# A hybrid layer on one core: linear attention placed between the last six in-projection slots, sliding attention within the first eight, gate sums ahead of them

## The chip, the core and the metric

The kernel runs on one core of a Trainium2 chip. Its engines run side by side, each through its own program in order, and meet in semaphores: TensorE multiplies matrices (its weight loads are a row of their own, PEld, in the profile), VectorE (DVE) and ScalarE (ACT) work elementwise, GpSimd (POOL) does a little elementwise work and issues transfers, SyncE (SP) issues transfers. The metric is the device time of one execution in microseconds (us), the median of the runs shown.

## What is computed

A block of two models. The first is one layer on 512 tokens of width 1024 whose mixer has three parts: sliding-window attention with 8 heads, an RWKV-7 recurrence with 4 heads, and gated linear attention with 4 heads. All three read the same normalised input. The second model, two more layers with full attention and feed-forward parts, is untouched here. Of the first layer's reference, what matters:

```python
h = _rmsnorm(x, g_pre) * (1.0 + scale[:, None]) + shift[:, None]
proj = h @ w_in                                   # 25 groups of 128 columns with the low-rank one
aq, ak, av, ag, rkv, rg, gq, gkk, gv, gg = jnp.split(proj, ...)
attn = _sliding_window_attention(aq, ak, av, sinks) * jax.nn.silu(ag)
rkv = rkv + (_shift(rkv) - rkv) * mu_rkv          # "token mix"
rwkv = _rwkv7_mixer(h, *jnp.split(rkv, 3, axis=-1), ...) * jax.nn.silu(rg)
gla = _gla_mixer(h, gq, gkk, gv, gk1, gk2, gk_b, gla_norm_w) * jax.nn.silu(gg)
y = jnp.concatenate([attn, rwkv, gla], axis=-1) @ w_out
return x + gate[:, None] * _rmsnorm(y, g_post)    # gate = c_act @ ada_w + ada_b, last third

# in _gla_mixer, for chunks of 64 tokens
b = jnp.cumsum(g_c, axis=2)
A = jnp.einsum('bhid,bhjd,bhijd->bhij', q_c, k_c, jnp.exp(diff))   # diff = b_i - b_j, causal
o = A @ v_c + jnp.einsum('bhid,bhdv->bhiv', q_c * jnp.exp(b), S)
```

## The kernel before

The whole program is one function, `build`, with a block of code for each engine. Nothing schedules it: the order on an engine is the order in which its block is written, and every meeting is a semaphore wait written by hand. Weights are full 32-bit numbers; each is split into a rounded high half and the rest (a low half), and each product is made of three matmuls (`three`, L2011 to L2013: high times high, high times low, low times high).

**The in-projection** has 24 slots after the low-rank one, of one weight tile of 128 columns each: `in1(item, g)` for g = 1 to 24. A slot is eight k-steps of three matmuls of 128x512. SyncE loads tiles into a ring (`refill`, L1947). ScalarE makes a tile's high half when the slot two before it is used (`ahead`, `weight_high`, L1203), VectorE then makes its low half (`weight_low`, L1490), and TensorE waits for that (`split_slot`). ScalarE also evacuates each slot's bank (`late` for the last fourteen, L2509); from item 17 on two banks take turns.

**Sliding attention** has 16 units u of a block of 128 queries and a pair of heads; the first four look at 128 keys, the others at 256. TensorE does `s1_step(u)`: transposes of unit u's probabilities (L2139), scores of unit u+1 (L2127), values of unit u-1 (L2153). Between, VectorE does `s1_max` (maximum L2823, then small operations to L2830), ScalarE `s1_exp` (L2559, L2561), VectorE `s1_normalise` (L2837 to L2840). `s1_gate` (L2846) takes the output. A step stands after every seventh k-step of slots 11 to 24. VectorE's loop over u also holds the low halves, the six token mixes (L2792, L2793; u = 2 to 7), the scan of the decay (L2865, u = 3) and the eight gate sums (`gate_sum`, L2801; u = 8 to 15), each over a tile of 512 KB that SyncE loads beside the ring's refills. A low half stands between the normalising of u and the maximum of u+1.

**Linear attention** is made in seven levels and a diagonal, since the decay between two tokens is a product of distances to the edges of blocks of 1, 2, 4, ... 64 tokens. For each level GpSimd computes distances (`g_distance`, L2442, L2443), ScalarE exponentiates them (`g_power`, L2582), VectorE multiplies queries and keys (`g_level`, L2877, L2878), TensorE makes 16 small matmuls of 32 rows, 4 chunks by 4 heads (`g_scores`, L2211; L2213 for the diagonal), and VectorE copies what belongs to the level under a mask (`g_take`, L2891; L2895 for the diagonal). Two sets of four PSUM banks take turns. Besides there are turned values and keys, chunk states (`g_state`), and the outputs in four blocks (`g_outputs`, L2225, L2228), which ScalarE copies (L2631). All of this stands behind the last slot. In its gaps stands **the recurrence's pointwise work** (key norms L2179, exponentials L2618, L2619, L2628, products L2947 to L2957). It ends in `r_inputs` 6, on which the recurrence's products wait (L2273), which VectorE masks in eight banks (`masked`, L2964).

The two lines that set the pace of steps and of late slots before:

```python
                if (at + k) % 7 == 6:                       # TensorE
                    s1_step((at + k) // 7)
            while 8 * split + 7 <= 7 * u + 6 and split < 14:   # VectorE, ahead of s1_max(u + 1)
                weight_low(ve, S_IN1 + 11 + split + SPLIT)
```

## Time and profile before

| | us |
|---|---|
| median of 3 runs | 1761.24 |
| lowest, highest | 1759.0, 1761.84 |
| the profiled execution | 1760.94 |
| its span | 1759.2 |
| its mean granted TensorE clock | 0.982 |

The profile is of one execution. Its times run from the span's start. The stretch that the change touches is from about 50 us (gate sums) and 106.4 us (slot 11) to about 271 us (the recurrence's level chain). "Released by" is inferred from semaphores. A TensorE row's busy time overlaps with its neighbours', so start to start is what a matmul takes in a row of them.

### The profile page before, as it was taken

The numbers are of one execution on the slowest core, as the hardware profiler recorded it, in microseconds if no ns is written. First come the engines' busy times: TensorE is split into PE (matmuls) and PEld (weight loads), VectorE is DVE, ScalarE is ACT, GpSimd is POOL, SyncE is SP. The second block draws the span as 40 slices with busy tenths as digits, with TensorE's granted clock in tenths as the row PEclk, the third lists the DMA queues.
The fourth block names the chain that finished last, engine by engine and source line by source line (L and its number), as shares of the span: only waits on it lengthen the run. The fifth ranks groups of instructions, "written<-read, shape, count | busy, mean of one in ns | idle before, by whom it ended". The sixth has DMA issues, their size and how long they took to land.

```text
span 1759.2 us, 32981 instructions
## 1 busy us (share of the span) xinstructions
PE 1701.1 (97%) x14287; PEld 1535.3 (87%) x14287; DVE 915.6 (52%) x1808; ACT 645.7 (37%) x1098; POOL 354.1 (20%) x466
## 2 busy tenths in 40 slices
PE   7999989989999999999999999999999999999997
PEld 3777779869988789999999998799769999999886
DVE  5347694445355654565652113788782556556002
ACT  3354442243145544222222224322683422222223
POOL 0001102001210012222222222343012222222221
PEclk9999979898999999999999999999999999999999
DMA  8521400126973358988889999699306888888996
GB/s 309 160 73 60 180 2 4 53 55 150 228 170 73 73 119 183 186 182 180 184 181 187 196 201 200 146 208 218 84 2 138 175 188 183 180 186 183 197 205 150
DMA packets 81648, 265.39 MB, mean 151 GB/s; under 512 B 11632, under 2 KB 15472, under 8 KB 81376
## 3 DMA queue, kind: packets, MB, share of 16 engines
q0 software_dynamic: 59040, 214.98, 57.7%
q1 hardware_dynamic: 18448, 42.52, 7.1%
q10 hardware_dynamic: 4016, 5.78, 1.1%
q8 instruction: 113, 1.85, 0.4%
q14 instruction: 31, 0.25, 0.0%
HBM read 251.44 MB, written 2.10 MB: 144 GB/s over the span
## 4 chain that ended last, share of the span: by engine, by line
PE 79%; DVE 3%; DMA 3%; ACT 2%; issue 1%; ACTq 0%; POOL 0%; DVEq 0%
PE banks L661 21%; PE banks L662 20%; PE banks L663 20%; PE banks L2273 3%; DMA w_lo<-in_weights 2%; PE banks L798 1%; DMA w_hi<-in_weights 1%; PE banks L729 1%; PE banks L713 1%; PE banks L2011 1%; PE banks L751 1%; PE banks L836 1%; PE banks L2013 1%; PE banks L2012 1%; PE banks L1072 1%
## 5 line engine op out<-in xcount | busy, mean ns | idle before, releaser
L661 PE MATMUL banks<-hn_hi,w_hi 128*128 128x264 f32 (+2 forms) x2168 | 624.7, 288 | 4.7 <-DMA w_lo<-in_weights 4.0
L662 PE MATMUL banks<-hn_lo,w_hi 128*128 128x264 f32 (+2 forms) x2168 | 617.1, 285 | 0.0
L663 PE MATMUL banks<-hn_hi,w_lo 128*128 128x264 f32 (+2 forms) x2168 | 616.4, 284 | 0.0
L1209 ACT ACTIVATE w_lo<-w_hi 128x1024 fp32r<-128x1024 f32 x202 | 214.1, 1060 | 720.5 <-DMA w_hi<-in_weights 712.5
L661 PEld LDWEIGHTS banks<-hn_hi,w_hi 128*128 128x128 f32 x2168 | 409.3, 189 | 17.0 <-issue 12.2
L662 PEld LDWEIGHTS banks<-hn_lo,w_hi 128*128 128x128 f32 x2168 | 410.4, 189 | 0.6 <-issue 0.2
L663 PEld LDWEIGHTS banks<-hn_hi,w_lo 128*128 128x128 f32 x2168 | 408.2, 188 | 0.3
L1154 POOL DMA_DIRECT2D w_hi<-in_weights x205 | 113.5, 554 | 881.2 <-PE banks L663 794.0
L1161 POOL DMA_DIRECT2D w_lo<-in_weights x205 | 183.2, 896 | 171.4 <-ACT w_lo L1209 122.2
L661 PE MATMUL banks<-a_hi,w_hi 128*128 128x264 f32 (+1 forms) x506 | 160.6, 317 | 1.9 <-DVE u_in L1758 0.8
L662 PE MATMUL banks<-a_lo,w_hi 128*128 128x264 f32 (+1 forms) x506 | 160.7, 318 | 0.0
L663 PE MATMUL banks<-a_hi,w_lo 128*128 128x264 f32 (+1 forms) x506 | 160.6, 317 | 0.0
L661 PEld LDWEIGHTS banks<-a_hi,w_hi 128*128 128x128 f32 x506 | 95.3, 188 | 9.7 <-DVE u_in L1758 1.0
L663 PEld LDWEIGHTS banks<-a_hi,w_lo 128*128 128x128 f32 x506 | 95.2, 188 | 6.7
L662 PEld LDWEIGHTS banks<-a_lo,w_hi 128*128 128x128 f32 x506 | 95.0, 188 | 6.6
L1758 DVE TENSOR_TENSOR u_in<-banks,rs 128x528 f32<-128x528 f32 x44 | 31.2, 708 | 98.3 <-PE banks L663 88.9
L1760 DVE TENSOR_TENSOR u_in<-banks,rs 128x516 f32<-128x516 f32 x44 | 30.6, 696 | 98.1 <-PE banks L663 91.3
L1490 DVE TENSOR_TENSOR ring_r<-ring,ring_r 128x1024 fp32r<-128x1024 f32 x32 | 39.6, 1238 | 76.5 <-ACT ring_r L1203 76.5
L2012 PE MATMUL banks<-h_r,ring_r 128*128 128x512 f32 x192 | 76.0, 396 | 0.0
L661 PE MATMUL banks<-o_hi,w_hi 128*128 128x264 f32 (+1 forms) x256 | 73.3, 286 | 1.3 <-DMA w_lo<-in_weights 0.7
L662 PE MATMUL banks<-o_lo,w_hi 128*128 128x264 f32 (+1 forms) x256 | 72.5, 283 | 0.0
L663 PE MATMUL banks<-o_hi,w_lo 128*128 128x264 f32 (+1 forms) x256 | 72.4, 283 | 0.0
(452 smaller groups left out, 2752.0 us busy)
## 6 DMA issues: line engine op xcount, KB each, us to landing
w_hi<-in_weights POOLq DMA_DIRECT2D x205, 512.0 KB, 5.2
w_lo<-in_weights POOLq DMA_DIRECT2D x205, 512.0 KB, 7.3
ring<-in_weights SPq DMA_DIRECT2D x48, 512.0 KB, 4.7
arena<-arena ACTq DMA_DIRECT2D x64, 66.0 KB, 5.4
arena<-arena SPq DMA_DIRECT2D x64, 66.0 KB, 4.0
arena<-in_gate_w SPq DMA_DIRECT2D x8, 512.0 KB, 3.5
h<-in_xT SPq DMA_DIRECT2D x2, 1024.0 KB, 6.4
arena<-in_alibi SPq DMA_DIRECT2D x1, 1024.0 KB, 6.4
```

The source lines that it names most:

```text
L661: mm(o, w[0][:, j, :], x[0][:, k, lo:hi], start=first, stop=False)
L662: mm(o, w[0][:, j, :], x[1][:, k, lo:hi], start=False, stop=False)
L663: ins_ = mm(o, w[1][:, j, :], x[0][:, k, lo:hi], start=False, stop=last)
L713: last = mm(psum[:, 2 * (v % 2) + c, at], qs[r, p, b * P:(b + 1) * P], kz[r, p, 0:keys(b)], start=True, stop=True)
L1154: g.dma_start(split_at(n)[0], ins["weights"][n]).then_inc(hi_loaded[w_turn(n)[0]], 16)
L1161: g.dma_start(split_at(n)[1], ins["weights"][n], accum_op=ALU.add).then_inc(lo_summed[w_turn(n)[0]], 16)
L1209: nc.scalar.activation(split_at(n)[1], split_at(n)[0].bitcast(F32), ACT.Copy, scale=-1.0).then_inc(S["w_negated"], 1)
L1490: nc.vector.tensor_tensor(ring_lo(n), ring_slot(n), ring_hi(n).bitcast(F32), ALU.subtract).then_inc(S["w_split_d"], 1)
L1758: V.tensor_tensor(halves(u_in[:, g % 4, 2:T2 + 2]), pair(g), rs2, ALU.mult).then_inc(S["u_evac"], 1)
L1760: V.tensor_tensor(halves(u_in[:, g % 4, KEEP + 2:T2 + 2]), kept_pair(g), halves(rs[:, KEEP:T2]), ALU.mult).then_inc(S["u_evac"], 1)
L2012: mm(out, w[0][:, k, :], x_lo, start=False, stop=False)
L2273: last = mm(out(s), lhs[r], rhs[r], start=start, stop=stop)
```

## The change

What it does:

- *TensorE:* an attention step stands after every fourth k-step, so that 16 steps end with slot 18 (`beside(p)`, p counts k-steps from slot 11). Between the k-steps of slots 19 to 24 stand the turned values and keys, the states, the key norms and their spreading, and the scores of each level, in two pieces of two heads each, one k-step apart (`G_SCORES_AT`). All levels use banks 0 to 3: a piece waits until the same heads of the level before are copied.
- *VectorE:* the attention loop keeps the maximum, normalising, gating, four token mixes (u = 3, 5, 7, 9), the scan (u = 4) and eight low halves, of which each stands ahead of every second maximum. Behind it come linear attention and the pointwise work with the six other low halves and two mixes between. `masked(0)` to `masked(3)` stand behind the norm of linear attention, since its output `g_o` now lies where the masked products go.
- *ScalarE:* five `g_power` in the loop (u = 8 to 12), the late slots' high halves and evacuations between the pointwise work, and both SiLU behind the last evacuation and ahead of the output copies.
- *GpSimd:* five distances as soon as the scan is there, instead of three; the zeroing behind the last maximum.
- *Gate sums:* VectorE does them beside the low halves of slots 1 to 10, and SyncE loads their tiles beside the refills there.
- *Layout:* several tiles move; the recurrence's v columns (two slots) are projected after q, k and v of linear attention.

The diff, cut:

```diff
-    ch = Carve(hn_raw, KT * (T2 + 1))
-    g_at = ch.take(4, T1)
-    g_kd = ch.take(T1)
-    g_o = ch.take(2, T1)
+    g_o = arena[:, front:front + 2 * T1].rearrange("p (j t) -> p j t", j=2)
...
+    BESIDE = 64
+    G_SCORES_AT = (67, 73, 78, 83, 88, 93, 98, 103)
...
         for n in range(S_IN1 + 6, S_IN1 + 10):
             refill(n)
+            if n > S_IN1 + 6:
+                gate_tile(n - S_IN1 - 7)
...
-        def g_scores(lv):
+        def g_scores(lv, pair):
...
-            elif lv:
-                pe.wait_ge(S["g_taken"], 2 * (lv - 1))
...
+            else:
+                pe.wait_ge(S["g_taken"], 2 * (lv - 1) + pair + 1)
             for c in range(4):
-                for hd in range(4):
+                for hd in (2 * pair, 2 * pair + 1):
...
+        def beside(p):
+            if p == 0:
+                s1_scores(0)
+            if p < BESIDE and p % 4 == 3:
+                s1_step(p // 4)
+            if p == 66:
+                s1_values(15)
+            if p in (68, 69):
+                g_values_turned(p - 68)
+            if p == 71:
+                g_keys_turned()
+            if p == 75:
+                g_states()
+            if p == 81:
+                key_norms()
+            if p == 92:
+                key_norms_spread()
+            for pair in range(2):
+                if p - pair in G_SCORES_AT:
+                    g_scores(G_SCORES_AT.index(p - pair), pair)
...
-        for lv in range(3):
+        for lv in range(5):
             g_distance(lv)
...
+        for j in range(11, 14):
+            late(j)
+        act.wait_ge(S["in1_evac"], ITEMS)
+        A(rgate, rgate, ACT.Silu)
+        A(ggate, ggate, ACT.Silu)
         for c in range(4):
             act.wait_ge(S["g_ops"], c + 1)
...
         for g in range(1, 7):
             weight_low(ve, S_IN1 + g + SPLIT)
+            if g >= 3:
+                gate_sum(g - 3)
...
-            while 8 * split + 7 <= 7 * u + 6 and split < 14:
+            while 8 * split + 7 <= 4 * u + 3:
                 weight_low(ve, S_IN1 + 11 + split + SPLIT)
...
-            if 2 <= u < 8:
-                token_mix(u - 2)
-            elif u >= 8:
-                gate_sum(u - 8)
+            if u in (3, 5, 7, 9):
+                token_mix((u - 3) // 2)
...
-        masked(0)
-        masked(1)
...
+        for b in range(4):
+            masked(b)
         first_level(0)
...
-        _groups(rkv), _groups(gq), _groups(gk), _groups(gv), _groups(rg), _groups(gg),
+        _groups(rkv[:, :512]), _groups(gq), _groups(gk), _groups(gv), _groups(rkv[:, 512:]), _groups(rg), _groups(gg),
```

TensorE, the scores of linear attention. Before, they stand behind the last slot, with nothing between the levels but their waits:

```order
L2211 MATMUL banks<-arena 128x64 x16
...
L2211 MATMUL banks<-arena 128x64 x16
...
L2211 MATMUL banks<-arena 128x64 x80
L2213 MATMUL banks<-arena 128x128 x16
```

In the changed kernel, a piece of eight stands between k-steps of three (L2024 to L2026 are the three matmuls, L2205 the scores, L2246 the states), here in slot 20:

```order
L2205 MATMUL banks<-arena 128x64 x8
L2024 MATMUL banks<-mix_r,ring_r 128x512
L2025 MATMUL banks<-h_r,ring_r 128x512
L2026 MATMUL banks<-mix_r,ring_r 128x512
L2205 MATMUL banks<-arena 128x64 x8
L2024 MATMUL banks<-mix_r,ring_r 128x512
L2025 MATMUL banks<-h_r,ring_r 128x512
L2026 MATMUL banks<-mix_r,ring_r 128x512
L2246 MATMUL banks<-arena 128x256 x3
```

A level's sixteen matmuls have become two pieces of eight between projection matmuls.

ScalarE, ahead of the output copies of linear attention. Before (L2621 the key factor, L2623 and L2624 the two SiLU, L2626 the square root, L2628 an exponential, L2631 the output copies):

```order
L2621 ACTIVATE arena<-arena,small,cols 128x512 x2
L2623 ACT_TABLE_LOAD
L2623 ACTIVATE arena<-arena 128x1024
L2624 ACTIVATE arena<-arena 128x1024
L2626 ACT_TABLE_LOAD
L2626 ACTIVATE arena<-arena 128x16
L2628 ACT_TABLE_LOAD
L2628 ACTIVATE arena<-arena 128x1024
L2631 ACTIVATE hn_raw<-banks 128x2x128 x4
```

In the changed kernel (L1210 a high half, L2544 an evacuation, L2662 the exponential, L2666 and L2667 the SiLU, L2670 the output copies):

```order
L2662 ACTIVATE arena<-arena 128x1024
L1210 ACTIVATE ring_r<-ring 128x1024
L2544 ACTIVATE arena<-banks 128x512
L1210 ACTIVATE ring_r<-ring 128x1024
L2544 ACTIVATE arena<-banks 128x512
L1210 ACTIVATE ring_r<-ring 128x1024
L2544 ACTIVATE arena<-banks 128x512
L2666 ACT_TABLE_LOAD
L2666 ACTIVATE arena<-arena 128x1024
L2667 ACTIVATE arena<-arena 128x1024
L2670 ACTIVATE arena<-banks 128x2x128 x4
```

The three last high halves and evacuations, and behind them both SiLU with a table load, now stand ahead of the output copies.

VectorE, ahead of a wide unit's maximum in the attention loop. Before, late in the loop (L1490 a low half, L2823 the maximum, L2846 the gate, L2801 a gate sum, L2837 the normalising):

```order
L1490 TENSOR_TENSOR ring_r<-ring,ring_r 128x1024
L2823 ISA arena,small<-banks,arena 128x256
L2823 ISA small 128x1
L2823 ISA arena,small<-banks,arena 128x256
L2823 ISA small 128x1
L2828 TENSOR_TENSOR small<-small,cols 128x2
L2829 TENSOR_TENSOR small<-cols,small 128x2
L2830 TENSOR_SCALAR small<-small 128x2
L2846 TENSOR_TENSOR arena<-banks,arena 128x128
L2801 ISA arena,ada<-arena 128x1024
L2801 ISA ada 128x1
L2837 TENSOR_TENSOR small<-small 128x2
```

In the changed kernel (L1497, L2867, L2890, then L2832 and L2833 the token mix, L2881 the normalising):

```order
L1497 TENSOR_TENSOR ring_r<-ring,ring_r 128x1024
L2867 ISA arena,small<-banks,arena 128x256
L2867 ISA small 128x1
L2867 ISA arena,small<-banks,arena 128x256
L2867 ISA small 128x1
L2872 TENSOR_TENSOR small<-small,cols 128x2
L2873 TENSOR_TENSOR small<-cols,small 128x2
L2874 TENSOR_SCALAR small<-small 128x2
L2890 TENSOR_TENSOR arena<-banks,arena 128x128
L2832 TENSOR_TENSOR rs<-arena 128x512
L2833 SCALAR_TENSOR_TENSOR arena<-rs,cols,arena 128x512
L2881 TENSOR_TENSOR small<-small 128x2
```

The low half still stands ahead of the maximum; the gate sum behind the gate has gone, and token mixes stand at u = 3, 5, 7, 9, which are units with a low half.

## Rows read from the trace of the kernel before

**Rows 1.** The page, part 1: busy time, share of span, instructions.

```profile
PE 1701.1 (97%) x14287; PEld 1535.3 (87%) x14287; DVE 915.6 (52%) x1808; ACT 645.7 (37%) x1098; POOL 354.1 (20%) x466
```

**Rows 2.** Windows by stage: window, length, busy of each engine, then granted clock, DMA.

```profile
106.80:215.80 109.00, 105.85 (x570) 79.48 (x569) 72.80 (x237) 52.34 (x131) 6.51 (x8) 1.00 0.31 106
215.80:248.70 32.90, 25.80 (x321) 22.55 (x321) 32.03 (x50) 18.62 (x25) 6.81 (x8) 0.59 0.05 19
...
216.00:218.00 2.00, 1.76 (x8) 1.36 (x7) 2.00 (x3) 0.99 (x2) 2.00 (x3) 0.50 0.70 256
```

**Rows 3.** Chain of waits behind the last slot: start, us, engine, tile, line.

```profile
215.77 1.21 DVE arena L2873
...
248.73 0.66 PE banks L2228 x8
...
256.03 1.68 PE banks L2179 x16
257.71 3.64 PE banks L2273 x64
...
265.98 2.41 DVE arena L2964 x4
```

**Rows 4.** Timeline of TensorE: attention steps and the slot behind one of them.

```profile
113.00 0.38 PE L2139 MATMUL banks<-ident,arena 128*128 128x128 f32 x2
...
118.73 0.38 PE L2139 MATMUL banks<-ident,arena 128*128 128x128 f32 x2
...
124.85 0.38 PE L2139 MATMUL banks<-ident,arena 128*128 128x128 f32 x2
...
137.60 0.66 PE L2139 MATMUL banks<-ident,arena 128*128 128x128 f32 x4 [0.23 <-DVE arena L2840]
...
157.64 0.60 PE L2139 MATMUL banks<-ident,arena 128*128 128x128 f32 x4
...
159.39 0.50 PE L2011 MATMUL banks<-mix_r,ring_r 128*128 128x512 f32 x1
...
164.40 0.60 PE L2139 MATMUL banks<-ident,arena 128*128 128x128 f32 x4
...
211.57 0.60 PE L2139 MATMUL banks<-ident,arena 128*128 128x128 f32 x4
```

**Rows 5.** Timelines of VectorE and ScalarE: one unit from slot end to normalised.

```profile
136.84 0.70 DVE L2840 TENSOR_SCALAR arena<-arena,small 128x256 f32<-128x256 f32 x1
...
157.89 1.06 ACT L1203 ACTIVATE ring_r<-ring 128x1024 fp32r<-128x1024 f32 x1 [2.74 <-PE banks L2013]
...
158.97 1.23 DVE L1490 TENSOR_TENSOR ring_r<-ring,ring_r 128x1024 fp32r<-128x1024 f32 x1 [2.42 <-ACT ring_r L1203]
160.12 0.42 DVE L2823 CUSTOM_DVE_ANT_0 arena<-banks,arena 128x256 f32<-128x256 f32 x1
...
162.40 0.19 ACT L2561 ACTIVATE small<-small 128x2 f32<-128x2 f32 x1
...
162.97 0.16 DVE L2837 TENSOR_TENSOR small<-small 128x2 f32<-128x2 f32 x1
...
163.64 0.35 DVE L2840 TENSOR_SCALAR arena<-arena,small 128x256 f32<-128x256 f32 x1
165.68 0.42 DVE L2823 CUSTOM_DVE_ANT_0 arena<-banks,arena 128x256 f32<-128x256 f32 x1 [1.69 <-PE banks L2127]
```

**Rows 6.** Timeline of TensorE: scores of two levels of linear attention.

```profile
227.47 1.12 PE L2211 MATMUL banks<-arena 32*128 32x64 f32 x32 [2.31 <-DVE arena L2907]
...
239.51 1.99 PE L2211 MATMUL banks<-arena 32*128 32x64 f32 x32 [1.28 <-DVE arena L2878]
```

**Rows 7.** Timeline of ScalarE: a SiLU, a table load, the first output copy.

```profile
236.24 1.04 ACT L2624 ACTIVATE arena<-arena 128x1024 f32<-128x1024 f32 x1
237.28 1.28 ACT L2626 ACT_TABLE_LOAD   x1
...
249.44 0.38 ACT L2631 ACTIVATE hn_raw<-banks 128x256 f32<-128x256 f32 x1 [8.28 <-PE banks L2228]
```

## What the rows before say of the change, and the prediction

> **What bounds the kernel now.** I read the page first. TensorE is busy for nearly the whole span [rows 1], so time is found only where it waits, or where it works on what could lie beside something else. The windows by stage come next [rows 2]: while the last fourteen in-projection slots run with sliding attention between them, TensorE is busy for 105.85 of 109 us at full clock. Then comes a stretch of 32.9 us in which VectorE is busy for 32.03, TensorE's granted clock averages 0.59 (0.50 in 216 to 218 us, the lower of its two levels), and no in-projection is left to fill its gaps. The chain of waits says the same [rows 3]: from 215.77 us it runs over VectorE's levels of linear attention, reaches the first output matmul at 248.73 and the recurrence's products at 257.71. Everything behind that point only shifts, except for one reordering priced below. So I compute when TensorE ends its last in-projection slot (call it S), when it reaches the products (before: 257.6), and what lies behind.
>
> **Sliding attention, from every 7 to every 4 k-steps.** Before, two steps stand 6.76 us apart (157.64 to 164.40): 1.75 for the step and 5.01 for 21 projection matmuls, 0.239 each [rows 4]. TensorE set that pace: with the same 6.76 fifteen times, 113.00 leads to 214.4 and the first, narrow ones to less: the last step starts at 211.57. After, 12 matmuls lie between: 1.75 + 12 x 0.239 = 4.61 us for a wide unit, and 1.1 + 2.87 = 3.97 for a narrow one (118.73 to 124.85 less 21 matmuls) [rows 4]. If TensorE still set the pace, 15 intervals would be 67 us instead of 98.6.
>
> But each step needs the probabilities of the scores that the step before issued. That chain is in the trace, link by link [rows 5]. *Even unit:* maximum starts 1.28 us after the step (164.40 to 165.68); maximum, exponentials and their end take 2.47 (160.12 to 162.59); normalising 1.02 (162.97 to 163.99); with hops 4.85 us. That is 0.24 over 4.61. *Odd unit:* now every odd step falls on a slot's end, and VectorE's program has the low half of a weight ahead of the maximum. It waits for ScalarE's high half, which waits for the slot. One such case is in the rows whole: slot end 157.64, high half 157.89, low half 158.97, maximum 160.12, normalised by 163.99: 6.4 us from slot end to next step, with one token mix in it; about 6.0 without a mix, and about 5.2 with a narrow unit (estimates from the same rows). TensorE has 4.6 us of work for that time. So each slot takes 4.61 + 6.4 = 11.0 us (10.6 without a mix) instead of 9.2.
>
> The sum: the first step cannot be earlier than before, 113.1, though only 12 matmuls are done by then (the first unit's probabilities set it: before they were ready about 1 us ahead of 113.00, and VectorE now has the last gate sum, 1.2 us, ahead of the first maximum). Units 0 to 3: 3.97 + 5.2 + 3.97 + 6.4 = 19.5. Six even units at 4.61 = 27.7, three odd with a mix at 6.4 = 19.2, two without at 6.0 = 12.0. Together 78.4. GpSimd now does five distance levels in this loop instead of three; beside the three, five of VectorE's operations took longer (the normalising at 136.84 took 0.70 instead of the 0.35 at 163.64), 1.65 us together by the same comparison over 4.7 us, and the step at 137.60 is the only one that TensorE waited for [rows 4, 5]. Five would cost 2.7, which this loop cannot hide. The last step starts at 113.1 + 78.4 + 2.7 = **194.2 us**, 17.4 earlier than 211.57, where 31 earlier was to be had.
>
> **The last six slots, with linear attention between.** TensorE's own work: the last attention step 1.1 and values 0.6; 48 k-steps of three matmuls at 0.239 = 34.4; eleven transposes in three pieces 1.6; states 1.35; column sums 1.8 (1.68 at 256.03 [rows 3]); spreading 1.1. The scores were 16 matmuls a level in one piece (32 records: 1.12 us where the clock was mostly high, 1.99 at the low level [rows 6]); they are now two pieces of half the heads each, with a re-entry of about 0.1 us. Ends: half of 1.12 plus 0.1 = 0.66, and 1.12 plus 0.1 if two heads overlap half as well as four. I take 0.8 for each of 14 pieces and 1.0 for the two on the diagonal: 13.2. Sum 55.15. VectorE's share does not fit worse: its 32.03 us [rows 2] plus six low halves of 1.15 and two mixes of 1.45 are 42. But all levels now use the same four banks, and the order is a strict alternation, so I also walked the queues: TensorE waits for level 1 of the operands (0.15), and for level 5's copies ahead of level 6's scores (about 1.0), since VectorE stands 2.3 us at the reciprocal (the square root is queued behind slot 21's evacuation and a table load) and 2.3 at the low half of slot 24. S = 194.2 + 55.15 + 1.2 = **250.6 us**. VectorE's last predicated copy ends at about 249.5, just earlier.
>
> The Trainium skill has a rule against this edit: "TensorE: Matmul & The Clock Gate", Part 3, says that a weight load overlaps running matmuls only where the row groups differ, and that four-row packing gives 3.07x. By it half the heads would lose half the overlap, every piece costs 1.22, and S is 5.9 us later. No row here shows two row groups of 32.
>
> **Outputs of linear attention.** Before, the outputs start at 248.73 and the products at 257.6, 8.9 us, with ScalarE idle and copying at once (249.44 [rows 7]). After, ScalarE has behind S, in its order: the high half of a weight and the evacuation (1.7 with the hop), a table load 1.28 and two SiLU of 1.04 [rows 7], and only then the first copy 0.38. Output blocks 2 and 3 wait for copies 0 and 1. So block 2 starts at S + 5.4, not S + 1.6; blocks 2 and 3 take 3.2, the bonus matmuls 1.9, the sums 1.8: the products start at S + 12.3 = **262.9**, 5.3 later than before. VectorE's rest (five operations of 1.15, one low half 1.15) ends at 257, not on the path. "ScalarE: Activation LUTs", What ACT_TABLE_LOAD costs, in the Trainium skill gives 2.66 us for a switch with its drain; here the load at 237.28 is 1.28 and stands directly behind the SiLU that ends there [rows 7]. The row decides; by the page the total would be 1.4 us higher.
>
> **Masked products.** Before, VectorE masks the first four banks while TensorE still makes products and spreads norms, and the chain then crosses VectorE, as at 265.98, where four masks are 2.41 [rows 3]. Linear attention's output now lies where the masked products go, so masks 0 to 3 stand behind its norm. VectorE is idle where they were, and four masks of 0.61 come onto the path: **+2.45 us**.
>
> **Gate sums early.** Eight sums of 1.2 us leave the attention loop, where VectorE had time, and eight loads of 512 KB go into SyncE's queue beside the first ten slots. Each weight there is ready a slot ahead and a slot is 5.6 us; I count nothing. If loads came late, the last sum alone would delay the first maximum, by 1 to 3 us.
>
> **Sum.** 5.3 + 2.45 = +7.7 us. The profiled execution took 1760.94, so 1768.6; against the median of 1761.24, 1768.9. A measurement of this kernel can tell some 0.2% (3.5 us) from no change.
>
> **Rivals.**
> *Attention keeps TensorE's pace (faster).* If the waits of odd and even units were absorbed, the loop would be 67 + 2.7 us and the last step at 183. The last six slots would stay at 56, and the total would be 11 us less: 1757.5. For it: before, TensorE waited once, for 0.23 us. Against: it had 5.7 us of other work behind each scores, and will have 3.4. It decides where slot end to probabilities is under 4.6 us; the row says 6.4. Chance 0.08, with all else that ends faster.
> *Gain and loss cancel (same).* The pieces of scores cost 0.66 (-2.2), GpSimd disturbs nothing (-2.7), and the walk's waits vanish (-1.2): +1.6, so 1763. Chance 0.19.
> *Half the heads, half the overlap.* 14 pieces at 1.22: +5.9, 1775. Chance 0.13.
> *The clock falls in the loop.* It fell after 212 us, where gaps of 1 to 2 us followed each other [rows 2]. The new waits are 1.8 us in 11, beside long dense runs, so I don't expect it; if it fell for two of the stretches of 4.6 us of work, each would double: +9, 1778. Chance 0.06.
> *Forecast:* 1769, between 1765 and 1772.5: chance 0.54.
>
> **How the numbers follow.** Slower by over 0.2% takes the forecast and the two worse rivals, 0.73; same 0.19; faster 0.08. The range leaves out most of the faster rival and the clock, and reaches from 1760.5 to 1776.
>
> **What would show it.** Right: in the profile after, slots with attention come 11.0 us apart, TensorE's waits in them end by VectorE's normalising, VectorE waits for ScalarE's high half ahead of every second maximum; the last attention step starts near 194; the last slot ends near 251; a SiLU stands ahead of the first output copy with TensorE idle 3.5 us; four masks follow the norm, with two gaps of 1.3 us on TensorE. Wrong: attention steps 4.6 us apart throughout; pieces of scores of 0.5 us or of 1.2; or S set by VectorE's queue, which would be so if its low halves wait longer than I walked.

## The result, and the profile after

| | median, us | runs | range | ratio to before, 95% interval |
|---|---|---|---|---|
| before, with one run more than above | 1760.38 | 4 | 1759.0 to 1761.84 | |
| after | 1790.31 | 4 | 1786.62 to 1795.24 | 1.0172 [1.0138, 1.0205] |
| after, a second time | 1786.06 | 4 | 1781.02 to 1789.46 | 1.0139 [1.0120, 1.0159] |

The change makes the kernel slower by 1.4 to 1.7%. The direction was forecast, the size was not: the +7.7 us of the sum stands against +25.7 in the profiled executions (1786.62 against 1760.94), and the time lies above the range. Nearly all of it arises between 100 and 300 us (1.3 us lie ahead of the first scores, experiment 7): where the recurrence's level chain starts on VectorE, after is 25.8 us behind before, and it is 25.7 behind at the end. This place, 1.5 ms ahead of the end, is therefore where the experiments are read: further down the same code can lose a few us in one execution and none in another. "At the level chain" below is that start against the trace of before: +25.8 for after, +24.9 for its second execution with a trace.

The page of after, part 1, answers to [rows 1]. TensorE is 14 us busier with the same 14287 instructions, so part of the loss is not waiting but slower work.

```profile
span 1784.8 us, 32988 instructions
...
PE 1715.1 (96%) x14287; PEld 1538.4 (86%) x14287; DVE 915.0 (51%) x1808; ACT 644.8 (36%) x1098; POOL 354.5 (20%) x466
```

TensorE's waits from 105 to 300 us in after: tile, line, what was waited for, sum, times, longest.

```profile
PE banks L2152 <- DVE arena L2884: 13.8, 9, 2.5
PE banks L2219 <- ACT arena L2670: 3.1, 1, 3.1
PE banks L2311 <- DVE arena L3020: 2.2, 2, 1.2
PE banks L2205 <- DVE arena L2930: 1.2, 1, 1.2
```

These are the four waits that the prediction walked out: attention's transposes behind VectorE's normalising, the third output block behind ScalarE's copy (behind the SiLU), the level chain behind masks, and one level's scores behind VectorE's copy. The windows of after, which answer to [rows 2], show what it did not count. Columns: window, length, busy of each engine, then granted clock of TensorE, DMA share, GB/s.

```profile
110.00:120.00 10.00, 7.98 (x33) 5.76 (x33) 4.84 (x25) 3.82 (x13) 0.00 (x0) 0.83 0.23 82
120.00:130.00 10.00, 8.74 (x50) 6.04 (x50) 4.96 (x25) 4.68 (x15) 0.00 (x0) 1.00 0.19 54
160.00:170.00 10.00, 9.16 (x49) 6.62 (x50) 4.67 (x19) 4.33 (x10) 0.00 (x0) 0.83 0.00 1
200.00:250.00 50.00, 48.84 (x399) 38.28 (x399) 35.05 (x53) 22.37 (x31) 2.96 (x4) 1.00 0.14 45
250.00:255.00 5.00, 5.00 (x25) 3.96 (x26) 2.95 (x5) 0.00 (x0) 0.00 (x0) 0.61 0.21 86
...
270.00:280.00 10.00, 8.66 (x36) 4.95 (x36) 1.71 (x2) 4.75 (x9) 0.00 (x0) 0.66 0.15 51
```

The clock leaves its high level (2.4 GHz) for the low one (1.2) for parts of the attention loop, of the last slots, and of the outputs. The timeline of TensorE shows how a fall begins. Here is one in the loop: start, us, engine, line, operation, and in brackets the idle time ahead of it with what ended it (matmul rows of a slot are L2024 to L2026, one of each three shown).

```profile
160.84 0.66 PE L2152 MATMUL banks<-ident,arena 128*128 128x128 f32 x4 [1.59 <-DVE arena L2884]
161.42 0.70 PE L2140 MATMUL banks<-arena 64*128 64x256 f32 x4
162.06 0.86 PE L2166 MATMUL banks<-arena 128*64 128x128 f32 x8
...
164.72 0.63 PE L2025 MATMUL banks<-h_r,ring_r 128*128 128x512 f32 x1
165.91 0.39 PE L2025 MATMUL banks<-h_r,ring_r 128*128 128x512 f32 x1
166.59 0.40 PE L2025 MATMUL banks<-h_r,ring_r 128*128 128x512 f32 x1
167.06 0.60 PE L2152 MATMUL banks<-ident,arena 128*128 128x128 f32 x4
```

After the wait of 1.59 us a projection matmul's row takes 0.63 instead of 0.39 for a few us, and the step-to-step interval is 6.22 (160.84 to 167.06) where the same work later in the loop takes 4.91 (173.46 to 178.37). Not every such wait is followed by a fall: in this trace the waits of 2.02 us ahead of 135.41 and of 1.60 ahead of 173.46 are not.

The interval of 4.91 is itself no pace of TensorE's. Its end, from the timelines of TensorE and VectorE:

```profile
173.46 0.66 PE L2152 MATMUL banks<-ident,arena 128*128 128x128 f32 x4 [1.60 <-DVE arena L2884]
...
177.93 0.40 PE L2026 MATMUL banks<-h_tail_r,ring_r 128*128 128x512 f32 x1
177.97 0.35 DVE L2884 TENSOR_SCALAR arena<-arena,small 128x256 f32<-128x256 f32 x1
178.37 0.66 PE L2152 MATMUL banks<-ident,arena 128*128 128x128 f32 x4
```

The transposes start 0.40 us behind the start of the last normalising, as they do where the profile lists a wait for it (194.54 to 194.95), and 0.44 behind the last projection matmul, where before has 0.24 (164.16 to 164.40). So VectorE's chain sets this interval too, by 0.2 us that the list of waits does not hold.

The last slots, TensorE's timeline: one early piece of scores with its neighbours, and the two around 250 us.

```profile
204.50 0.40 PE L2026 MATMUL banks<-mix_r,ring_r 128*128 128x512 f32 x1
204.83 1.11 PE L2205 MATMUL banks<-arena 32*128 32x64 f32 x16
205.86 0.50 PE L2024 MATMUL banks<-h_tail_r,ring_r 128*128 128x512 f32 x1
...
206.67 0.60 PE L2231 MATMUL banks<-ident,arena 128*128 128x128 f32 x4
...
248.81 1.11 PE L2205 MATMUL banks<-arena 32*128 32x64 f32 x16 [1.16 <-DVE arena L2930]
...
250.74 1.66 PE L2205 MATMUL banks<-arena 32*128 32x64 f32 x16
...
252.92 0.63 PE L2025 MATMUL banks<-h_r,ring_r 128*128 128x512 f32 x1
```

One matmul is two rows of the record (x16 is eight calls); the counts here and in the expectations are records. Sixteen records of two heads take 1.11 us at full clock; [rows 6] had 1.12 for 32 of four heads. With the gap ahead of it (in a run the next matmul would start 0.24 behind 204.50, at 204.74, and not at 204.83) and the slower k-step behind it (205.86 to 206.67 is 0.81, where three matmuls in a run take 0.70), a piece costs 1.03 + 0.09 + 0.11 = 1.23 us, not the 0.8 that the sum had.

The stretch behind the last slot, ScalarE's timeline and then TensorE's:

```profile
267.71 1.28 ACT L2666 ACT_TABLE_LOAD   x1
269.01 1.06 ACT L2666 ACTIVATE arena<-arena 128x1024 f32<-128x1024 f32 x1
269.97 1.04 ACT L2667 ACTIVATE arena<-arena 128x1024 f32<-128x1024 f32 x1
270.92 0.64 ACT L2670 ACTIVATE arena<-banks 128x256 f32<-128x256 f32 x2
```

```profile
266.00 0.66 PE L2222 MATMUL banks<-arena 128*64 128x128 f32 x8
...
271.34 0.58 PE L2219 MATMUL banks<-arena 128*128 128x128 f32 x2 [3.10 <-ACT arena L2670]
...
281.05 3.71 PE L2311 MATMUL banks<-arena 64*64 64x128 f32 x64
...
291.88 2.08 PE L2311 MATMUL banks<-rmask,arena 64*64 64x64 f32 x64 [1.16 <-DVE arena L3020]
295.00 2.08 PE L2311 MATMUL banks<-rmask,arena 64*64 64x64 f32 x64 [1.04 <-DVE arena L3020]
```

Before needs 8.9 us from the first output to the products; this needs 15.05.

So the theory to test has four separate causes: the attention loop's chain (waits, and the clock after them), the pieces of half the heads, the SiLU in front of the output copies, and the late masks. Its rivals: that the falls of the clock have another origin than TensorE's standing still; that a piece is dear because it stands between projection matmuls, not because it has two heads; that the early gate tiles disturb the loads; and that undoing one cause only makes the next one bind.

### The profile page after: what moved, and what is told of

Its sections match the earlier page's. It is cut to its first block, busy times and chain, and to the rows that moved or that the text cites. A ratio compares the mean times of both kernels' runs of the same rounds, so it can differ in the third digit from the quotient of the medians.

```text
span 1784.8 us, 32988 instructions
## 1 busy us (share of the span) xinstructions
PE 1715.1 (96%) x14287; PEld 1538.4 (86%) x14287; DVE 915.0 (51%) x1808; ACT 644.8 (36%) x1098; POOL 354.5 (20%) x466
## 4 chain that ended last, share of the span: by engine, by line
PE 89%; DVE 4%; ACT 3%; DMA 2%; issue 1%; SPq 0%; ACTq 0%; POOL 0%; DVEq 0%
PE banks L668 21%; PE banks L669 20%; PE banks L670 20%; PE banks L2024 3%; PE banks L2311 3%; PE banks L2025 3%; PE banks L2026 3%; PE banks L805 1%; PE banks L736 1%; PE banks L720 1%; PE banks L758 1%; PE banks L843 1%; PE banks L2205 1%; DMA ring<-in_weights 1%; PE banks L1079 1%
## 5 line engine op out<-in xcount | busy, mean ns | idle before, releaser
L1497 DVE TENSOR_TENSOR ring_r<-ring,ring_r 128x1024 fp32r<-128x1024 f32 x32 | 39.7, 1239 | 80.7 <-ACT ring_r L1210 80.7
```

The source lines that it names most:

```text
L1497: nc.vector.tensor_tensor(ring_lo(n), ring_slot(n), ring_hi(n).bitcast(F32), ALU.subtract).then_inc(S["w_split_d"], 1)
```

## The experiments

### 1. VectorE's order in the attention loop

```diff
-            while 8 * split + 7 <= 4 * u + 3:
-                weight_low(ve, S_IN1 + 11 + split + SPLIT)
-                split += 1
             if u + 1 < 16:
                 s1_max(u + 1)
+            while 8 * split + 7 <= 4 * u + 3:
+                weight_low(ve, S_IN1 + 11 + split + SPLIT)
+                split += 1
...
-            if u in (3, 5, 7, 9):
-                token_mix((u - 3) // 2)
+            if u in (2, 6, 8, 10):
+                token_mix((2, 6, 8, 10).index(u))
```

> Kernel after, with the attention loop on VectorE changed in two orders: the low half of a slot stands behind the maximum of the next unit instead of in front of it, and the four token mixes stand in units 2, 6, 8 and 10 instead of 3, 5, 7 and 9. Theory A (the chain through the unit is late because 1.2 us of low half and 1.4 us of token mix lie in front of the next maximum): the nine waits on normalised probabilities, 13.8 us in the trace of after, fall under 3 us, the granted clock of the loop goes back to 1.00, which gives back about 4 us more, and the time falls by 12 to 15, from 1786.6 to about 1773. Rival B (the waits only follow ScalarE, whose half of the work is as full in odd units): the waits move from VectorE's product to ScalarE's exponential or copy, and the time stays within 4 us of 1786.6. Rival C (the clock in the loop falls for another reason than the waits): the waits go but the clock stays at .7 to .87 in the same stretches, and the time falls by 8 to 10.

Measured: 1775.82 us (ratio 1.0082 [1.0055, 1.0109]). The waits in the trace:

```profile
PE banks L2152 <- DVE arena L2884: 5.6, 8, 1.9
PE banks L2219 <- ACT arena L2670: 3.1, 1, 3.1
```

From 13.8 us to 5.6, and the last attention step starts at 189.45 instead of 199.86. From step 7 on, the interval behind an odd step falls from 6.40 or 5.84 to 4.91, the same as behind an even one, and the clock falls only once in the loop. At the level chain the shift is 15.0, 10.8 less. (The profiled execution, 1780.79 us, was the slowest of the four: it lost 6.5 us more between 550 and 725 us, in the second model.) Theory A holds; 5.6 us of waits are more than the 3 it allowed, since the first units and those beside GpSimd's distances still wait (intervals of 5.42 and 6.08). The edit moves two things, and no run moves one alone; behind steps 11 and 13, where neither kernel has a token mix in the unit, 5.84 becomes 4.91 by the low half's place.

### 2. Scores of a level in one piece

```diff
-            for pair in range(2):
-                if p - pair in G_SCORES_AT:
-                    g_scores(G_SCORES_AT.index(p - pair), pair)
+            if p in G_SCORES_AT:
+                g_scores(G_SCORES_AT.index(p))
```

(and `g_scores` loops over four heads, waiting for both copies of the level before).

> Kernel after, with each level's scores of linear attention as one piece of 32 matmuls of four heads (it waits for both copies of the level before) at the position where the first half stood, instead of two pieces of 16 matmuls of two heads. Theory A (matmuls overlap by the number of heads in a run: two heads cost 1.04 to 1.11 us for 16, four heads 1.12 us for 32): eight pieces of about 1.12 instead of sixteen of 1.04 to 1.11, and eight re-entries into the projection fewer, so 8 to 9 us less, from 1786.6 to about 1778, if the wait for both copies is hidden. Rival B (a piece costs by its number of matmuls when it stands between projection matmuls): a piece of 32 costs about 2.1, and the time stays at 1786 +-1. Rival C (the wait for both copies is not hidden): pieces of 1.12, but a wait of up to 1.3 us in front of most, which takes the gain back, 1784 to 1788.

Measured: 1775.57 us (1.0098 [1.0070, 1.0125]). TensorE's timeline:

```profile
202.32 1.12 PE L2205 MATMUL banks<-arena 32*128 32x64 f32 x32
...
240.07 1.73 PE L2205 MATMUL banks<-arena 32*128 32x64 f32 x32 [1.75 <-DVE arena L2929]
242.32 0.63 PE L2025 MATMUL banks<-h_r,ring_r 128*128 128x512 f32 x1
```

32 records of four heads take what 16 of two took. The last attention step to the first output takes 57.44 us (197.38 to 254.82) instead of 66.14 in after, 8.7 less, although the one wait grew from 1.16 to 1.75; eight pieces of 1.23 saved would be 9.8. B falls: the neighbours are the same here. A's size holds. What it is in two heads that makes them dear stays open in one point: each head has its own rows of the array and its own PSUM bank, so a run of two heads is also a run of two banks, here and in experiment 3, and no run tells the two apart. C is seen in one piece of eight.

### 3. The same question without projection matmuls

```diff
-            for c in range(4):
-                for hd in range(4):
+            for c, hd in [(c, hd) for pair in range(2) for c in range(4) for hd in (2 * pair, 2 * pair + 1)]:
```

> Kernel before with each level's 32 scores in another order: first the sixteen of heads 0 and 1, then the sixteen of heads 2 and 3; the same matmuls, and no projection between them. Theory A (runs of two heads overlap half as much as runs of four): the pieces of 32 take 2.0 to 2.2 us instead of 1.12, 7 to 8 us more over the eight levels, of which part lies in the 5 us that TensorE waits there: 1763 to 1768. Rival B (what makes the pieces of two heads dear is that they stand between projection matmuls): 1.12 us as before, and 1759 to 1762.

Measured, one run: 1769.01 us, at the level chain +4.5. The pieces of 32 in its timeline, to set beside [rows 6]:

```profile
228.38 2.89 PE L2211 MATMUL banks<-arena 32*128 32x64 f32 x32 [2.31 <-DVE arena L2907]
...
240.13 2.89 PE L2211 MATMUL banks<-arena 32*128 32x64 f32 x32 [0.68 <-DVE arena L2878]
```

```profile
215.80:248.70 32.90, 27.84 (x271) 25.39 (x275) 28.06 (x43) 18.62 (x25) 6.82 (x8) 0.50 0.05 20
```

The order of heads alone makes a piece dearer, so B falls a second time. The size is not the expected one: the whole stretch ran at the low level (0.50, where before had 0.59), and there it is 2.89 against 1.99, a factor of 1.45; at the high level experiment 2 shows a factor of two. The piece at 227.47 in before ran at 1.12, and its counterpart here at 2.89, so part of the +4.5 is clock. The trace of experiment 7, with the order of before, was at the low level there too (0.52): its level chain is 2.4 us late, 1.2 of which it had at the first scores. About 1.2 us of the +4.5 may so be clock, and about 3.3 the order (an estimate from these shifts).

### 4. SiLU behind the squares

```diff
-        act.wait_ge(S["in1_evac"], ITEMS)
-        A(rgate, rgate, ACT.Silu)
-        A(ggate, ggate, ACT.Silu)
         for c in range(4):
...
             A(g_o_sq(j), g_o[:, j, :], ACT.Square).then_inc(S["g_osq"], 1)
+        act.wait_ge(S["in1_evac"], ITEMS)
+        A(rgate, rgate, ACT.Silu)
+        A(ggate, ggate, ACT.Silu)
```

> Kernel after, with ScalarE's two SiLU behind the four output copies and the two squares instead of in front of them. Theory A (the 3.1 us wait of TensorE for ScalarE's output copy, and the low clock behind it, are the two SiLU and their table load): the wait goes, the products start 12 to 13 us behind the last projection matmul instead of 15.1, and the time falls by 2.5 to 5, to about 1783. Rival B (the SiLU then stand in the way of the square roots and of the gated outputs): the outputs run on, but TensorE waits as long before it spreads the variances, and the time is 1786.6 +-1. Rival C (the clock behind the last slot stays low for another reason): the wait goes, the clock stays near .66, and the gain is 1 to 2.

Measured: 1779.67 us (1.0107 [1.0086, 1.0127]). First output to products:

```profile
268.06 0.49 PE L2219 MATMUL banks<-arena 128*128 128x128 f32 x2
...
271.21 1.98 PE L2300 MATMUL banks<-arena 128*128 128x512 f32 x4
273.03 1.84 PE L2180 MATMUL banks<-arena 128*128 128x2 f32 x16
274.80 3.71 PE L2311 MATMUL banks<-arena 64*64 64x128 f32 x64
```

From 265.90 to 274.80 is 8.9 us, exactly before's. The edit gives 6.15 us, more than A's upper end: 3.1 of wait and 3 of work that ran at the low level behind it (in after the bonus matmuls, L2300, took 2.91, here 1.98). The granted clock from 270 to 280 us is 1.00 here. All six traces with the wait of 3.1 us have a low stretch behind it (granted clock 0.50 to 0.66 in its slowest 5 us); the four without the wait, this one and those of experiments 9 and 10, have none. The square roots come later and nobody waits for them, and B falls, and C with the clock.

### 5. Masks back between the steps of the norm

```diff
-    g_o = arena[:, front:front + 2 * T1].rearrange("p (j t) -> p j t", j=2)
+    g_o = hn_raw[:, 5 * T1:7 * T1].rearrange("p (j t) -> p j t", j=2)
...
-        for b in range(4):
-            masked(b)
```

(with `masked(0)` to `masked(3)` where they stood before).

> Kernel after, with the output of linear attention in the space it had in the kernel before, and so the first four masks of the products back between the steps of its normalisation. Theory A (the masks stand late and hold up the level chain by 2.45 us, as forecast; TensorE's waits of 1.16 and 1.04 us for the masks are that): both waits go and the time falls by 2.0 to 2.6, to about 1784.3. Rival B (the gated outputs are then late by as much, and TensorE waits for them instead): 1786.6 +-1.

Measured: 1780.40 us (1.0117 [1.0095, 1.0139]), more than expected. TensorE's timeline says why:

```profile
247.76 1.11 PE L2205 MATMUL banks<-arena 32*128 32x64 f32 x16 [1.16 <-DVE arena L2930]
249.68 1.11 PE L2205 MATMUL banks<-arena 32*128 32x64 f32 x16
...
286.65 4.00 PE L2311 MATMUL banks<-rmask,arena 64*64 64x64 f32 x128
```

Both waits for masks are gone (the last row runs through, where after has two gaps), and from first output to level chain the edit gives 2.2 us, as in A. The other 4.2 us arose ahead of the edit: the loop lost 1 us less to the clock, and the wait of 1.16 at 247.76, the same as in after, was followed by no fall (1.11 at 249.68, where after has 1.66 at 250.74). Of the six traces with this wait of 1.16, this is the one without a fall behind it, and so it prices that fall: from the wait to the first output it takes 14.1 us (247.76 to 261.85), after 17.2 (248.81 to 266.00) for the same work, 3.1 more.

### 6. Work for TensorE in the waits of the loop

```diff
+            if u % 2 == 0 and 2 <= u:
+                pe.wait_ge(S["s1_soft"], u + 1)
+                for _ in range(4):
+                    mm(psum[:, 2 * (u % 2) + 1, 256:512], ident[:, :], q1[:, 0, 0:256], start=True, stop=True)
             pe.wait_ge(S["s1_prob"], u + 1)
```

> Kernel after, with four matmuls of 256 columns (0.4 to 0.5 us each by the rate of the 512-column ones) on TensorE in front of the transposes of the seven later even units, into a part of a bank that nobody reads: they run where TensorE waits for the normalised probabilities, and change nothing else. Theory A (the clock falls because TensorE stands still in those waits): the granted clock of the loop stays at .95 to 1.00 in 110 to 200 us (.94 in after), the slots' twelve matmuls go back to 2.9 us each, and the last unit's step starts 3 to 4 us earlier than in after (199.86), for the filler fits in the waits of 0.8 to 2.6 us, but for the shortest. Rival B (the clock falls for another reason, or at the rate of its own): the clock stays .94 and the filler costs what does not fit in the waits, 1 to 4 us more.

Measured beside the second run of after: 1778.20 against 1786.06 us (ratios 1.0100 [1.0085, 1.0116] and 1.0139 [1.0120, 1.0159]). The window of the loop, where after has 0.94:

```profile
110.00:200.00 90.00, 85.81 (x473) 62.32 (x473) 54.95 (x212) 41.98 (x118) 9.75 (x11) 1.00 0.16 50
```

With seven groups of four useless matmuls the program is faster. The filler (1.89 us for a group) is longer than most waits, so the intervals behind odd steps grow (5.84 to 6.43), and yet the last step starts 2.6 us earlier measured from the first scores, since the intervals of 5.18, 6.18 and 6.22 become 3.87, 4.91 and 4.85. The first of the three is not the filler's: no filler stands ahead of it, the wait ahead of it is 1.94 us (2.02 in after), and experiment 2 has 3.86 there without any filler.

For the other two, one trace would not do, since a fall can also stay out by itself. All traces together do better. From 125 to 200 us the five with after's order of VectorE and no filler (after twice, experiments 2, 4 and 5) have one or two falls each, each behind a wait of 1.59 to 2.70 us; the five in which these waits are filled or gone (this one, and experiments 1, 9 twice and 10) have none. So theory A holds for the loop: what goes ahead of a fall is TensorE standing still. The gain at the end is larger than in the loop and in part unexplained: at the level chain the shift is 24.2 (25.8 and 24.9 in the traces of after), the two profiled executions end 3.4 us apart, the medians 7.9.

### 7. The gate sums early, alone

The kernel before, with only the eight gate tiles and sums moved as in the change.

```diff
         for g in range(1, 7):
             weight_low(ve, S_IN1 + g + SPLIT)
+            if g >= 3:
+                gate_sum(g - 3)
```

> Kernel before with one part of the change alone: the eight gate tiles and their sums early, among the first slots of the in-projection, instead of in the last units of the attention loop. Theory A (as forecast, harmless: they lie in VectorE's free time): within 0.2% of before, 1758 to 1764, and the first attention scores start at 108.25 +-0.3. Rival B (the gate tiles' transfers compete with the ring's, and the 1.3 us that all traces of after are late by at the first scores is theirs): the first scores start at 109.5 and the time is 1.3 us longer, less what the free VectorE gives back in the loop.

Measured over 12 runs: 1760.09 us (0.9993 [0.9981, 1.0004]). No difference, as forecast. Its trace has the first scores 1.2 us late, like the first trace of after; but the second trace of after, with the same gate tiles, is 0.2 late. The 1.3 us arise near 20 us: of two products of the first weights (16 records each) one takes 1.9 us and one 3.3 to 3.6. Where the scores are early (before, the second trace of after) the slow one is the first, at 17.2 to 17.4 us; where they are late (after, this trace) it is the second, at 22.2 to 22.3. Both happen to one kernel, so this belongs to the execution, not to the change.

### 8. After again

> The kernel after as it is, beside the others on one chip. Every theory expects 1786 to 1795 us, 1.4% to 2.0% over before; a difference between this run and the first one bounds what the comparisons can tell, and its trace shows which of the stretches with a low clock come again: those behind the waits of the attention loop and of the last slots should, by the theory that waits bring them, and those further down need not.

Measured: 1786.06 us, the lower end of what was expected. The waits are the same to 0.1 us, and the low stretches are the same ones, 110 to 120 (0.83), 160 to 170 (0.83), 250 to 255 (0.50), 270 to 280 (0.66).

### 9. The four edits together

Experiments 1, 2, 4 and 5 in one kernel.

> Kernel after with the four single edits together: low half and token mix behind the next maximum, scores as one piece of four heads, SiLU behind the squares, first four masks back between the steps of the normalisation. At the start of the recurrence's level chain the four edits alone moved the shift against before from 25.8 us to 15.0, 14.7, 19.6 and 19.4, of which the edit itself made 12, 11, 6 and 2.2. Theory A (they are separate causes): the shift becomes 25.8 - 31 = -5, and the time is 1754 to 1758, under the kernel before. Rival B (the stages share one slack: with the loop 12 us earlier, the last slots and VectorE's takes become the bound): the sum is cut by 6 to 10, and the time is 1760 to 1766.

Measured: 1754.85 us, **0.9963 [0.9948, 0.9978]**, and a second time:

> The kernel with the four edits again, beside the one with five, on one chip: 1751 to 1758, a ratio to before of 0.995 to 0.998. It bounds how well two kernels 2 us apart can be told apart.

Measured: 1752.08 us, **0.9943 [0.9928, 0.9959]**. This kernel keeps the change's overlap of stages, without its cut of the scores in two and its late masks, and is faster than before by 0.4 to 0.6%. Its waits and windows:

```profile
PE banks L2152 <- DVE arena L2883: 5.7, 8, 1.9
PE banks L2205 <- DVE arena L2929: 1.8, 1, 1.8
```

```profile
110.00:200.00 90.00, 84.06 (x520) 58.28 (x519) 61.72 (x225) 46.46 (x128) 11.80 (x15) 1.00 0.18 53
200.00:250.00 50.00, 47.87 (x423) 36.88 (x422) 39.82 (x56) 22.45 (x31) 0.00 (x0) 1.00 0.20 64
250.00:300.00 50.00, 49.43 (x1525) 48.68 (x1526) 26.16 (x40) 15.34 (x26) 13.40 (x10) 1.00 0.02 4
```

The level chain starts 7.6 us earlier than before (3.6 in the second trace, where the clock fell once in the loop and once among the slots). A expected 5: the causes are separate, and B falls. That 25.8 became -7.6 and not -5 is within what the clock does from one trace to the next: the 4.0 us between the two traces are 1.2 at the first scores, 1.3 in the loop and 1.5 behind the wait of 1.75 in the slots.

### 10. One order more

`g_take(5)` ahead of `beside_low(11)` on VectorE, in the kernel of experiment 9.

> The kernel with the four edits, and one more: VectorE copies the sixth level's scores before it takes the low half of the slot that stood in front of that copy. Theory A (the one wait left in the last six slots, 1.75 us for that copy, which stood behind a low half that itself waited 3.35 us for ScalarE): the wait goes and the time falls by 1.5 to 2, to 1752 to 1754 where the four edits gave 1754.85. Rival B (the low half is then late for its slot): a new wait of TensorE for the ring, and no gain.

Measured: 1751.99 us, 0.9947 [0.9933, 0.9962], beside 1752.08 for the same kernel without it. The wait of 1.8 us is gone from the trace and no wait for the ring takes its place; last attention step to first output takes 52.5 us instead of 54.3. In the time the two cannot be told apart.

## Why the prediction was wrong in size

Predicted and measured, in its own steps (us, first profiled execution of after):

| step | predicted | measured | what made the difference |
|---|---|---|---|
| first attention step | 113.1 | 114.35 | the execution: 113.29 in the second trace |
| from there to the last step | 81.1 | 85.5 | clock +3.9, even intervals +1.8, GpSimd -1.2 |
| last six slots, to S | 56.35 | 66.1 | pieces +6.6, clock +3.1 |
| S to the products | 12.3 | 15.05 | clock +3.0 |
| masks | +2.45 | +2.4 | |
| total | +7.7 | +25.7 | |

**The chain of the attention loop was right, but for one step of its sum.** The odd interval with a token mix was given as 6.4 us and is 6.40; without one 6.0 and is 5.84. The wait ended by VectorE's normalising, with ScalarE's high half and VectorE's low half ahead of the maximum, is in the trace as described, and experiment 1 removes it. Two small sizes were off against each other. The even wide interval is 4.91 and not 4.61: the prediction had found a chain of 4.85 us through VectorE there, 0.24 over TensorE's 4.61, and then summed 4.61; the chain is what counts, and over six intervals this is 1.8 us. The intervals beside GpSimd's five distances are 1.5 us over the pattern (5.42 and 7.43 where it has 4.91 and 6.40), not 2.7; that GpSimd is the cause rests on the time at which they fall alone.

**The term that failed first: the pieces of scores.** The sum took 0.8 us for half a level, a value between "all of the overlap kept" (0.66) and "half of it" (1.22). Half of it is what the traces show: the piece costs 1.23, as the third rival had it. Fourteen pieces are 6.0 us over the sum, and the two on the diagonal (1.09 and the same two additions, 1.29 and not 1.0) make it 6.6. I gave that rival 0.13 since no row of before showed two heads in a run. The Trainium skill, "TensorE: Matmul & The Clock Gate", Part 3, says that a weight load overlaps running matmuls only where the row groups differ. The traces do not contradict it, but it does not give the factor by itself: neighbouring matmuls differ in their row group in both orders, and 16 records in two groups still take 1.11 us, 32 in four 1.12.

**The step that failed next: the clock.** The fourth rival was right in mechanism and its chance of 0.06 was wrong. I argued that waits of 1.8 us among dense work would not bring the clock down. They did, for three of the loop's intervals (5.18, 6.18 and 6.22, where 3.87, 4.91 and 4.91 are the same work at full clock), once behind 1.16 us in the slots, and behind 3.1 us at the outputs: 3.9 + 3.1 + 3.0 = 10.0 us in all, against the 9 that the rival had, which placed them all in the loop. Experiments 1 and 6 with the other traces show the cause for the loop, experiment 4 for the outputs. For the slots it rests on the timelines: no run took away that wait alone with pieces as in after. Nor does a wait always bring a fall: the same one did in one execution and did not in another.

Both rivals held together: 7.7 + 5.9 + 9 = 22.6 of the 25.7 us. They were priced apart, as alternatives to one another, and the range, to 1776, took in the one with the pieces (1775) and neither the one with the clock (1778) nor the two together, although nothing in the one excludes the other. That is why the measured time lies beyond the upper end. The other 3.1 us are small terms: the first step 1.25 late, the clock and the pieces 1.0 and 0.7 over what the rivals had, the even intervals less GpSimd's part 0.6, less some tenths elsewhere.

**The rest held.** Gate sums: harmless (experiment 7). SiLU ahead of the copies: 3.5 us of idle time forecast, 3.10 measured. Masks: 2.45 forecast, two gaps of 1.16 and 1.04 seen where two of 1.3 were announced. The wait for one level's copies: about 1.0 forecast, 1.16 measured.

**The faster rival** (attention keeps TensorE's pace) fell for this kernel, but mostly for a reason that a change of VectorE's order removes. I treated the low half's place ahead of the maximum as given. With all four edits the same overlap of stages gains 6 to 10 us over before. Even then TensorE's pace of 4.61 is not reached: the intervals are 4.91, VectorE's chain.

## What to carry to other kernels

When a stage is packed tighter between other work, follow each engine's program order around the chain that gets shorter cover: here one weight split in front of a maximum, and two SiLU in front of four copies, cost more than the overlap gained. Price each short wait of TensorE twice, once as the wait and once as the work behind it that may run at half the clock. And do not cut a run of small matmuls in four row groups into runs of two: keep all groups in the run, even if a buffer must be waited for. Last, where a chain was found longer than an engine's own work, put the chain into the sum, however small the difference, and price rivals that do not exclude each other together as well.

## What the runs showed of the hardware

- Sixteen records of matmuls over 32 rows in two row groups take 1.11 us, 32 in four row groups 1.12, at full clock. At the low level 32 take 2.89 us in runs of two groups and 1.99 in runs of four. Two groups were also two PSUM banks in each run, four groups four.
- Falls of TensorE's clock followed waits of 1.16 to 3.1 us inside otherwise dense work and lasted a few us. They cost 1.3 us behind a wait in the loop, 1.5 to 3.1 in the slots and 3.0 at the outputs. A wait did not always bring one: behind 3.1 us it came in six of six traces, behind the 1.16 in five of six, behind the 1.75 in two of three (of the two traces of experiment 9, one kernel, in one), and waits of 2.02 and 1.60 us in after's loop passed without. It is likely, but not shown, that this is why executions of after spread from 1781 to 1795 us.
- Matmuls whose results nobody reads, placed in the waits, made the program 8 us faster in the median of four runs; the trace shows 2.6 us of it in the loop, of which 1.3 are not the filler's, and 3.4 at the end beside the second trace of after.
